# Attention in half-steps, and another order for the last expert group and the final norm

## The chip, the cores and the metric

The kernel runs on one core of a Trainium2 chip. The metric is the device time of one execution in microseconds. TensorE does the matrix products (PE in the rows, PEld for its weight loads), VectorE is DVE, ScalarE is ACT, GpSimd is POOL, and SyncE (SP) issues nearly all transfers. Each engine works through its own instructions in order and waits on semaphores for the others.

## The reference

A trunk of two layers over 256 tokens and 16 meta tokens of width 1024, in float32. Layer 0 mixes with a gated convolution and linear attention, layer 1 with grouped-query attention. Each layer ends with 32 experts, of which each token uses two, and after the last layer comes an RMS norm:

```python
def attend_block(q_blk, k, v):
    s = jnp.einsum('bqhgd,bkhd->bhgqk', q_blk, k) * (ATT_HEAD_DIM ** -0.5)
    p = jax.nn.softmax(s, axis=-1)
    return jnp.einsum('bhgqk,bkhd->bqhgd', p, v)
...
    for e in range(N_EXPERTS):
        he = jax.nn.silu(xt @ w_gate[e]) * (xt @ w_up[e])
        out = out + gates[:, e:e + 1] * (he @ w_down[e]).astype(jnp.float32)
...
    return rms_norm(h, norm_final)
```

Layer 1 has 16 query heads and 4 key heads of 64; its queries are the 256 real tokens, its keys all 272. Each expert has three matrices of 1 MB.

## The kernel before

Tokens lie in three tiles: tile 0 has the 16 meta tokens, tiles 1 and 2 have 128 tokens each. `h` (the residual) and `hn` are [128, 3, 1024] in SBUF. There are eight PSUM banks, `B[0]` to `B[7]`.

**Attention of layer 1** goes over eight pairs of heads `p`. For each pair there are two query tiles `i` and two heads `o`, so four score tiles [128, 272], one in each of `B[0]` to `B[3]`. The four engines' programs are written apart and meet in semaphores:

- TensorE: `att_scores(p)` (L1913) makes the four score tiles, each when `p_exp` says that the exponentials of the pair before have left its bank. `turn_probs(p)` (L1926, L1933) transposes the divided probabilities into `B[4]`, `B[5]` and, for the meta keys, `B[6]`. `att_values(p)` (L1947, L1951) multiplies them with the values into `B[7]`. The loop's order is scores of p+1, turns of p, values of p-1.
- VectorE: `maxima(p)` takes four row maxima (L1324) and, for each tile of queries, scales them (L1328, `s_max`). `invert(p)` inverts the four sums of exponentials (L1334) and multiplies the four tiles of probabilities (L1338, `p_ready`). `meta_out(p)` copies the turned meta part (L1344), `oT_low(p)` makes the low part of the output (L1348). The order is maxima of p+1, low part of p-2, division of p+1, meta part of p. `qT_out(1)`, the copy of the second half of the turned queries (L1315), stands after the first division.
- ScalarE: `exps(p)` makes the four exponentials with their sums (L832), `pT_out(p)` evacuates the turned probabilities (L841), `oT_out(p)` the output (L845). The order is exponentials of p+1, turned probabilities of p, output of p-1.

The output projection follows when the last `oT_low` is done.

**Experts.** `moe(l)` serves both layers. It works on eight groups `q` of four experts, 32 token slots to an expert. For a group TensorE makes the gate and the up product (`gate_up`, L1711), ScalarE takes silu (L733), VectorE multiplies (L1192), TensorE transposes (L1737), ScalarE evacuates (L735), TensorE makes the down product (`down`, L1748), and both halves of its columns are evacuated as `y` (L739 and L1205). `scatter` (L1800) brings a group's result back to the tokens by a product for each half of columns and each tile, and VectorE's `add_tokens` adds it to `h` (L1172, semaphore `h_added`). The products of the scatter use two banks in turn, so each waits for the add two before it. The scatter of a group comes inside the next group; in the last group (`last_quad`) it stands behind the transposes of the last group's product. Scatters go over half 0 of all tiles, then half 1. In layer 0 there are three tiles, so six products and adds, in layer 1 two tiles and four. Each product is two matmuls in the trace.

**Weights.** SyncE issues one transfer for each matrix, through 18 slots of 1 MB, in the fixed order gate, up, down of each group. The four gate matrices of a group are one stage, the four up matrices another, the four down matrices a third. A slot is filled again when `stage_done` says that its last reader is done. For layer 1 the first three transfers are issued when the query projection is done; the next eight wait for

```python
                sp.wait_ge(sem("oT_ps"), 8)
                for i in range(3, 11):
                    unit(1, i)
```

that is, for the last product with the values. After each layer's first round of experts every engine reads how many more rounds there are (`more_rounds`, none here) and branches past their code; on TensorE that branch stands ahead of `last_quad`.

**Final norm** (`norm(4)`). ScalarE squares each tile of `h` over all 1024 columns with a sum (L543) when the tile's last add is done (`wait_h`), VectorE takes the mean and adds epsilon (L869), ScalarE takes the root (L532), VectorE inverts it (L877) and scales the tile by it and by the gain (L887); SyncE stores each tile (L451).

Of the kernel before, what the change touches and what calls it, by code (L numbers as in the profile page):

```python
# [5 lines left out]
def build_program(nc: bass.Bass, A: dict, out: bass.AP):  # L6
# [9 lines left out]
    P = 128  # L16
# [76 lines left out]
    with ctx:  # L93
# [38 lines left out]
        eps_var = sb("eps_var", [P, 3])  # L132
        idx_g = sb("idx_g", [P, 3, 8], u32)
# [205 lines left out]
        def _(sp):  # L339
# [162 lines left out]
        def wait_h(eng, n, i, steps):  # L502

            tiles = len(NORM_TILES[n - 1]) if n else 3
            if n == 0:
                eng.wait_ge(sem("h_in"), 48)
            elif n in (1, 3):
                eng.wait_ge(sem(f"h_mixed{n // 2}"), [3, 2][n // 2] + i + 1)
            else:
                eng.wait_ge(sem(f"h_added{n // 2 - 1}"), steps * NQ * 2 * tiles + (NQ - 1) * 2 * tiles + tiles + i + 1)  # L510
# [8 lines left out]
        def _(act):  # L519
            link = chain(act, "act_chain")  # L520

            def norm(n, steps=None):
# [23 lines left out]
                if n % 2:  # L546
# [276 lines left out]
            def exps(p):  # L823
                for i in range(2):
                    for o in range(2):
                        at = 16 + 16 * (p // 4) + 8 * i + 2 * (p % 4) + o
                        k = 4 * p + 2 * i + o
                        if o == 0:
                            act.wait_ge(sem("s_max"), 2 * p + i + 1)
                        if p >= 2 and i == 0 and o == 0:  # L830
                            act.wait_ge(sem("pT_ps"), 3 * (p - 1))
                        nc.scalar.activation(probs[:, 4 * (p % 2) + 2 * i + o, :], B[2 * i + o][:, 0:T], ACT.Exp,  # L832
                                             bias=att_max[:, k:k + 1], scale=hstat[:, 3, at:at + 1],
                                             accum_out=att_sum[:, k:k + 1]).then_inc(sem("p_exp"), 1)
# [27 lines left out]
        def _(dve):  # L862
# [16 lines left out]
            def scale_tile(n, i):  # L879
# [4 lines left out]
                if i == 0:  # L884
                    dve.wait_ge(sem("gain_in"), {0: 16, 4: 32}[n])
                gain = gain_last if n else gain_first
                nc.vector.scalar_tensor_tensor(hn[0:m, t, :], h[0:m, t, :], stats[0:m, n, 3, t:t + 1], gain[0:m, :],  # L887
                                               ALU.mult, ALU.mult).then_inc(sem("hn_ready"), 1)

            def norm(n):  # L890
                tiles = len(NORM_TILES[n])
                mean_square(n, 0)
                for i in range(tiles):
                    if i + 1 < tiles:
                        mean_square(n, i + 1)
                    scale_tile(n, i)
# [19 lines left out]
            link(nc.vector.memset(hn[:, 0, :], 0.0))  # L916
            nc.vector.memset(stats[:, :, :, :].rearrange("p a b c -> p (a b c)"), 1.0).then_inc(sem("clear"), 1)

            nc.vector.memset(z[:, :, :].rearrange("p a b -> p (a b)"), 0.0).then_inc(sem("clear"), 1)
            norm(0)  # L920
# [144 lines left out]
            def moe(l):  # L1065
# [99 lines left out]
                def add_tokens(base, q):  # L1165

                    for k in range(nadd):
                        half, t = k // NT, tiles[k % NT]
# [13 lines left out]
                def one_round(r, first):  # L1182
# [136 lines left out]
            def maxima(p):  # L1319
                for i in range(2):  # L1320
                    for o in range(2):
                        k = 4 * p + 2 * i + o
                        dve.wait_ge(sem("s_ps"), k + 1)
                        last = nc.vector.tensor_reduce(att_rcp[:, k:k + 1], B[2 * i + o][:, 0:T], X, ALU.max, negate=True)  # L1324
                    link(last)
                    at = 16 + 16 * (p // 4) + 8 * i + 2 * (p % 4)
                    k = 4 * p + 2 * i
                    nc.vector.tensor_tensor(att_max[:, k:k + 2], att_rcp[:, k:k + 2], hstat[:, 3, at:at + 2], ALU.mult).then_inc(sem("s_max"), 1)  # L1328

            def invert(p):  # L1330
                k = 4 * p
                dve.wait_ge(sem("p_exp"), 4 * p + 4)
                dve.wait_ge(sem("s_max"), 2 * p + 2)
                nc.vector.reciprocal(att_rcp[:, k:k + 4], att_sum[:, k:k + 4]).then_inc(sem("p_rcp"), 1)  # L1334
                dve.wait_ge(sem("p_rcp"), p + 1)
                for x in range(4):
                    pr = probs[:, 4 * (p % 2) + x, :]
                    nc.vector.tensor_scalar(pr, pr, att_rcp[:, 4 * p + x:4 * p + x + 1], None, ALU.mult).then_inc(sem("p_ready"), 1)  # L1338
# [677 lines left out]
```

## Time and profile before

| | us |
|---|---|
| median of 3 runs | 763.95 |
| lowest and highest | 762.96, 767.34 |
| the profiled execution, its own time | 761.59 |
| its span, first to last instruction | 759.7 |

In the profiled execution TensorE was busy for 646.2 us (85% of the span), VectorE for 250.0, ScalarE for 172.8, GpSimd for 61.4. The transfers moved 233.91 MB, 308 GB/s on average. The mean granted TensorE clock was 0.937. Times in the rows are counted from the start of the span. In a timeline row the first number is the start, the second the time to the end of the merged instructions, and a square bracket at the end says how long the engine had been idle and what released it. Busy times are of one engine; they overlap those of others, so their sum says nothing.

### The profile page before, as it was taken

To read this page: it belongs to the slowest core of one execution; us is meant where nothing else is said; L and a number is where in the kernel's file an instruction comes from. 1 tells how busy PE (TensorE), PEld (TensorE's weight loads), DVE (VectorE), ACT (ScalarE), POOL (GpSimd) and SP (SyncE) were. 2 spreads that over 40 slices of the span, in tenths; PEclk is the share of its full clock that TensorE was granted. 3 is DMA by queue.
4 is the path that set the end of the run, shared out by engine and by line. 5 is a ranking of instruction groups with operands and counts; after the bars stand their busy time and mean duration, and the time that the engine had idled before them with its cause. 6 is when DMAs were issued, how large, how long until landed. Compare 5 with 4: busy or idle time off the path is not lost.

```text
span 759.7 us, 10990 instructions
## 1 busy us (share of the span) xinstructions
PE 646.2 (85%) x4720; PEld 398.5 (52%) x4720; DVE 250.0 (33%) x575; ACT 172.8 (23%) x354; POOL 61.4 (8%) x43
## 2 busy tenths in 40 slices
PE   3999999988899998699589988787899787686674
PEld 3896987346566373374224345466566353244231
DVE  5255434133122332033043677713213221211204
ACT  5653350031200010010005346713111000000002
POOL 4222260000000000000003420000000000000000
PEclk9999999997999999699799999999899988888888
DMA  9760345991999999999994322069999999999991
GB/s 300 272 219 1 125 125 176 374 421 62 408 422 402 423 420 421 422 420 422 417 395 156 112 75 92 1 198 424 368 424 420 420 421 421 421 420 421 421 392 63
DMA packets 45753, 233.91 MB, mean 308 GB/s; under 512 B 4432, under 2 KB 4688, under 8 KB 23168
## 3 DMA queue, kind: packets, MB, share of 16 engines
q1 hardware_dynamic: 44864, 232.34, 76.5%
q0 software_dynamic: 832, 0.76, 0.7%
q8 instruction: 41, 0.67, 0.4%
q14 instruction: 16, 0.13, 0.0%
HBM read 232.02 MB, written 1.05 MB: 307 GB/s over the span
## 4 chain that ended last, share of the span: by engine, by line
PE 66%; DMA 18%; DVE 6%; SPq 4%; ACT 3%; issue 2%; DVEq 0%; ACTq 0%
PE bank L1711 11%; DMA ring<-in_moe_w_up 10%; PE bank L1775 8%; DMA tail<-in_moe_w_up 7%; PE bank L1800 7%; PE bank L1748 5%; PE bank L1408 5%; PE bank L1409 4%; PE bank L1410 4%; PE bank L1762 4%; SPq L370 4%; PE bank L1617 4%; PE bank L1863 4%; ACT scratch L832 2%; PE bank L1870 1%
## 5 line engine op out<-in xcount | busy, mean ns | idle before, releaser
L1711 PE MATMUL bank<-ring,hnT 128*32 128x256 f32 (+1 forms) x1616 | 141.5, 462 | 56.5 <-DMA ring<-in_moe_w_up 24.8
L1711 PEld LDWEIGHTS bank<-ring,hnT 128*32 128x32 f32 x1616 | 70.7, 128 | 120.8 <-issue 50.9
L1800 PE MATMUL bank<-moe_scratch 128*128 128x512 f32 (+1 forms) x160 | 78.1, 611 | 1.8 <-ACT moe_scratch L739 1.6
L1192 DVE TENSOR_TENSOR moe_scratch<-moe_scratch,bank 128x256 f32<-128x256 f32 x16 | 6.7, 421 | 182.4 <-ACT moe_scratch L733 182.4
L1172 DVE TENSOR_TENSOR h<-bank,h 128x512 f32<-128x512 f32 (+1 forms) x80 | 55.1, 689 | 23.7 <-PE bank L1800 23.7
L1775 PE MATMUL bank<-sel,hn 128*128 128x256 f32 x240 | 59.1, 406 | 0.0
L1748 PE MATMUL bank<-ring,moe_scratch 128*32 128x512 f32 x496 | 58.2, 595 | 0.3 <-ACT moe_scratch L735 0.3
L1775 PEld LDWEIGHTS bank<-sel,hn 128*128 128x128 f32 x240 | 58.0, 337 | 0.0
L1800 PEld LDWEIGHTS bank<-moe_scratch 128*128 128x128 f32 (+1 forms) x160 | 22.7, 169 | 50.3 <-issue 26.3
L1408 PE MATMUL bank<-hnT_hi,mix_hi 128*128 128x272 f32 x160 | 47.1, 294 | 1.7 <-DVE scratch L1016 1.7
L733 ACT ACTIVATE moe_scratch<-bank 128x256 f32<-128x256 f32 x16 | 6.1, 384 | 186.0 <-PE bank L1711 186.0
L1409 PE MATMUL bank<-hnT_hi,mix_lo 128*128 128x272 f32 x160 | 46.3, 289 | 0.0
L1711 PE MATMUL bank<-tail,hnT 128*32 128x256 f32 (+1 forms) x304 | 46.1, 433 | 0.0
L1410 PE MATMUL bank<-hnT_lo,mix_hi 128*128 128x272 f32 x160 | 46.0, 288 | 0.0
L1762 PE MATMUL bank<-sel,hn 128*128 128x128 f32 (+1 forms) x120 | 30.5, 421 | 2.1 <-DVE sel L1122 2.1
L1408 PEld LDWEIGHTS bank<-hnT_hi,mix_hi 128*128 128x128 f32 x160 | 30.3, 189 | 3.6 <-DVE scratch L1016 2.0
L1762 PEld LDWEIGHTS bank<-sel,hn 128*128 128x128 f32 x120 | 29.2, 335 | 5.6 <-issue 5.6
L1410 PEld LDWEIGHTS bank<-hnT_lo,mix_hi 128*128 128x128 f32 x160 | 30.2, 189 | 0.0
L1409 PEld LDWEIGHTS bank<-hnT_hi,mix_lo 128*128 128x128 f32 x160 | 30.2, 189 | 0.0
L307 POOL TENSOR_TENSOR mix_lo<-ring,mix_hi 128x2048 fp32r<-128x2048 f32 x5 | 24.0, 4800 | 69.8 <-ACT mix_hi L586 69.8
L1748 PEld LDWEIGHTS bank<-ring,moe_scratch 128*32 128x32 f32 x496 | 14.9, 109 | 26.8 <-issue 26.0
L739 ACT ACTIVATE moe_scratch<-bank 128x512 f32<-128x512 f32 x16 | 9.6, 597 | 84.8 <-PE bank L1748 84.8
(291 smaller groups left out, 852.0 us busy)
## 6 DMA issues: line engine op xcount, KB each, us to landing
ring<-in_moe_w_down SPq DMA_DIRECT2D x62, 1024.0 KB, 25.9
ring<-in_moe_w_up SPq DMA_DIRECT2D x48, 1024.0 KB, 24.2
ring<-in_moe_w_gate SPq DMA_DIRECT2D x46, 1024.0 KB, 22.1
ring<-in_sc_w_in SPq DMA_DIRECT2D x12, 1024.0 KB, 12.5
tail<-in_moe_w_gate SPq DMA_DIRECT2D x10, 1024.0 KB, 26.2
tail<-in_moe_w_up SPq DMA_DIRECT2D x8, 1024.0 KB, 25.4
ring<-in_moe_w_gate SPq DMA_DIRECT2D x14, 512.0 KB, 9.3
ring<-in_moe_w_up SPq DMA_DIRECT2D x14, 512.0 KB, 10.1
```

The source lines that it names most:

```text
L370: sp.dma_start(dst.rearrange("p (c n) -> p c n", c=KC), src).then_inc(sem(f"weights{l}_{stage_of(i) % NSEM}"), 16)
L1172: nc.vector.tensor_tensor(hh, B[[7, 4][k % 2]][0:n, :], hh, ALU.add).then_inc(sem(f"h_added{l}"), 1)
L1408: mm(dst, left[0], right[0], start=start, stop=False)
L1409: mm(dst, left[1], right[0], start=False, stop=False)
L1410: return mm(dst, left[0], right[1], start=False, stop=stop)
L1617: last = mm(bank[:, :], hnT[:, c, TILE_AT[t]:TILE_AT[t] + P], out_weights(half, c), start=(c == 4), stop=(c == 3))
L1711: return mm(bank[at, :], xT[:, c, mine], right, start=(c == 0), stop=(c == KC - 1))
L1748: last = mm(B[5 + half][at, :], heT[:, c, at], w[j][:, c * D + half * W:c * D + half * W + W], start=(c == 0), stop=(c == 1))
L1762: last = mm(B[k][:, width * cc:width * cc + width], hn[:, t, c:D:KC], picks, start=(t == a), stop=(t == b - 1))
L1775: last = mm(B[k % 2][:, 2 * P * cc:2 * P * cc + 2 * P], hn[:, t, c:D:KC], picks, start=(t == a), stop=(t == b - 1))
L1800: mm(B[[7, 4][k % 2]][0:m, :], selgT[:, TILE_AT[t]:TILE_AT[t] + m], y[:, half, :], start=True, stop=True).then_inc(sem(f"sc_ps{l}"), 1)
L1863: last = mm(bank[:, :], hnT[:, c, TILE_AT[t]:TILE_AT[t] + P], att_weights(2 * b + c // 4)[:, c % 4 * W:c % 4 * W + W], start=(c == 0), sto ...
```

## The change

Attention's steps are cut in two, one half for each tile of queries: `exps(p, i)`, `maxima(p, i)`, `normalize(p, i)` (the former `invert`, now with a reciprocal for each half) and `att_scores(p, i)`. Each engine's loop is written in another order around them. In the last expert group of both layers the scatter of the group before stands between the gate and the up product, its adds stand ahead of the product of silu and up, and the last group's scatter goes tile by tile. The final norm works in halves of 512 columns: squares, scaling and stores; epsilon and the division by 1024 move into the root.

```diff
@@ SyncE, output
             for i in range(2):
-                sp.wait_ge(sem("hn_ready"), HN_BEFORE[4] + i + 1)
-                sp.dma_start(out[0, i * P:(i + 1) * P, :], hn[:, 1 + i, :]).then_inc(sem("out_done"), 16)
-            sp.wait_ge(sem("out_done"), 32)
+                for half in range(2):
+                    cols = slice(half * W, half * W + W)
+                    sp.wait_ge(sem("hn_ready"), HN_BEFORE[4] + 2 * i + half + 1)
+                    sp.dma_start(out[0, i * P:(i + 1) * P, cols], hn[:, 1 + i, cols]).then_inc(sem("out_done"), 16)
+            sp.wait_ge(sem("out_done"), 64)
@@ all engines
+        def scattered(q, tiles):
+            if q < NQ - 1:
+                return [(half, t) for half in range(2) for t in tiles]
+            return [(half, t) for t in tiles for half in range(2)]
@@ ScalarE, final norm
+                if n == 4:
+                    done = steps * NQ * 4 + (NQ - 1) * 4
+                    for i, t in enumerate(tiles):
+                        for half in range(2):
+                            act.wait_ge(sem("h_added1"), done + 2 * i + half + 1)
+                            cols = slice(half * W, half * W + W)
+                            nc.scalar.activation(hn[:, t, cols], h[:, t, cols], ACT.Square,
+                                                 accum_out=(stats[:, 4, 0, t:t + 1], half_ss[:, t:t + 1])[half]).then_inc(sem("norm_ss"), 1)
+                            if i == 1:
+                                act.wait_ge(sem("norm_var"), upto(4) + half + 1)
+                                of = slice(tiles[half], tiles[half] + 1)
+                                nc.scalar.activation(stats[:, 4, 2, of], stats[:, 4, 1, of], ACT.Sqrt,
+                                                     bias=eps_bias[:, 0:1], scale=1.0 / D).then_inc(sem("norm_std"), 1)
+                    return
@@ ScalarE, attention
-            exps(0)
+            exps(0, 0)
+            exps(0, 1)
             qT_out(1)
             for p in range(8):
-                if p < 7:
-                    exps(p + 1)
-                pT_out(p)
                 if p:
                     oT_out(p - 1)
+                if p < 7:
+                    exps(p + 1, 0)
+                pT_out(p)
+                if p < 7:
+                    exps(p + 1, 1)
@@ VectorE, final norm
+                total(0)
+                invert_root(4, 0)
+                dve.wait_ge(sem("gain_in"), 32)
+                scaled(0, 0)
+                total(1)
+                scaled(0, 1)
+                invert_root(4, 1)
+                scaled(1, 0)
+                scaled(1, 1)
@@ VectorE, experts
                     for q in range(NQ):
+                        if q == NQ - 1:
+                            add_tokens(base, q - 1)
                         dve.wait_ge(sem(f"silu{l}"), base + q + 1)
                         nc.vector.tensor_tensor(he, act_g, B[2][:, F:2 * F], ALU.mult).then_inc(sem(f"he{l}"), 1)
-                        if q:
+                        if 0 < q < NQ - 1:
                             add_tokens(base, q - 1)
@@ VectorE, attention
-            maxima(0)
+            maxima(0, 0)
+            maxima(0, 1)
             query_rotate(1, 1)
             query_scale(1)
-            invert(0)
-            qT_out(1)
             for p in range(8):
+                normalize(p, 0)
+                if p:
+                    meta_out(p - 1)
                 if p < 7:
-                    maxima(p + 1)
-                if p >= 2:
-                    oT_low(p - 2)
+                    maxima(p + 1, 0)
+                normalize(p, 1)
+                if p == 0:
+                    qT_out(1)
+                if p:
+                    oT_low(p - 1)
                 if p < 7:
-                    invert(p + 1)
-                meta_out(p)
-            oT_low(6)
+                    maxima(p + 1, 1)
+            meta_out(7)
             oT_low(7)
@@ TensorE, last expert group
-                    gate_up(r, q)
+                    gate_up(r, q, (0,))
+                    scatter(r, q - 1)
+                    gate_up(r, q, (1,))
                     he_transposes(r, q)
-                    scatter(r, q - 1)
                     transpose_weights(r, q)
@@ TensorE, attention
             for p in range(8):
                 if p < 7:
-                    att_scores(p + 1)
-                turn_probs(p)
+                    att_scores(p + 1, 0)
                 if p:
                     att_values(p - 1)
+                if p < 7:
+                    att_scores(p + 1, 1)
+                turn_probs(p)
             att_values(7)
```

In the final norm `total` adds the two halves' sums of squares and `scaled` scales one half of a tile's columns. `wait_h` for the transposes after layer 0 asks for the adds of whole tiles in the new order.

## Rows read from the trace of the kernel before

**Rows 1.** The page, part 2: DMA busy in tenths of 40 slices.
```profile
DMA  9760345991999999999994322069999999999991
```

**Rows 2.** Timeline: first division, seventh product and evacuation, queue's restart.
```profile
457.56 1.18 DVE L1338 TENSOR_SCALAR scratch<-scratch,att_rcp 128x272 f32<-128x272 f32 x4
...
495.79 1.08 PE L1947 MATMUL bank<-scratch 128*64 128x256 f32 x8
...
497.36 0.38 ACT L845 ACTIVATE hnT_hi<-bank 128x256 fp32r<-128x256 f32 x1 [1.31 <-PE bank L1951]
...
499.81 0.33 SPq L367 DMA_DIRECT2D ring<-in_moe_w_gate  x1
```

**Rows 3.** Timeline of one attention step, by engine.
```profile
475.32 0.58 ACT L832 ACTIVATE scratch<-bank,att_max,scratch 128x272 f32<-128x272 f32 x1 [1.42 <-DVE att_max L1328]
...
477.56 1.09 ACT L841 ACTIVATE scratch<-bank 128x512 f32<-128x512 f32 x2
...
477.70 0.18 DVE L1334 RECIPROCAL att_rcp<-att_sum 128x4 f32<-128x4 f32 x1 [1.19 <-ACT scratch L832]
477.92 1.18 DVE L1338 TENSOR_SCALAR scratch<-scratch,att_rcp 128x272 f32<-128x272 f32 x4
479.01 0.41 DVE L1344 COPY scratch<-bank 64x256 f32<-64x256 f32 x1
479.34 0.77 DVE L1324 TENSOR_REDUCE att_rcp<-bank 128x1 f32<-128x272 f32 x2
...
480.23 0.78 DVE L1324 TENSOR_REDUCE att_rcp<-bank 128x1 f32<-128x272 f32 x2
...
479.15 1.09 PE L1926 MATMUL bank<-consts,scratch 128*128 128x128 f32 x8
...
481.59 1.08 PE L1947 MATMUL bank<-scratch 128*64 128x256 f32 x8 [0.78 <-DVE hnT_lo L1348]
```

**Rows 4.** Busy us in attention: PE, PEld, DVE, ACT, POOL, then clock, DMA.
```profile
470.00:480.00 10.00, 8.43 (x74) 5.36 (x72) 7.41 (x27) 7.20 (x22) 0.00 (x0) 1.00 0.00 0
```

**Rows 5.** Timeline, layer 0's last expert group and the work after it.
```profile
377.20 0.64 PE L1711 MATMUL bank<-ring,hnT 128*32 128x256 f32 x2 [3.45 <-DMA tail<-in_moe_w_up]
...
383.58 5.82 PE L1800 MATMUL bank<-moe_scratch 128*16 128x512 f32 x12
...
390.72 0.64 PE L1748 MATMUL bank<-ring,moe_scratch 128*32 128x512 f32 x4
...
407.16 0.29 DVE L1229 TENSOR_TENSOR hnT<-bank,gain_att 128x128 f32<-128x128 f32 x1 [5.46 <-issue]
```

**Rows 6.** Layer 0's last down issue: start, and time to landing.
```profile
L373 SPq DMA_DIRECT2D ring<-in_moe_w_down x1: 2143/2143/2143, 359.7 to 359.7; - x1
...
DMA to landing us min/median/max: 27.4/27.4/27.4
```

**Rows 7.** Timeline of TensorE, layer 1's last up and down products.
```profile
731.34 5.35 PE L1711 MATMUL bank<-ring,hnT 128*32 128x256 f32 x64 [3.96 <-DMA ring<-in_moe_w_up]
...
742.93 3.64 PE L1748 MATMUL bank<-ring,moe_scratch 128*32 128x512 f32 x32
```

**Rows 8.** Chain of waits: an up product warm (start us, us, what).
```profile
585.17 3.50 PE bank L1711 x64
```

**Rows 9.** Stretch in layer 1's last up product, same columns.
```profile
731.50:732.00 0.50, 0.50 (x8) 0.22 (x4) 0.00 (x0) 0.00 (x0) 0.00 (x0) 0.50 1.06 442
```

**Rows 10.** Layer 1's last two down issues: starts, and time to landing.
```profile
L373 SPq DMA_DIRECT2D ring<-in_moe_w_down x2: 436/1283/2130, 710.9 to 713.1; - x2
...
DMA to landing us min/median/max: 27.0/27.5/28.0
```

**Rows 11.** Timeline of VectorE in the final norm.
```profile
752.49 0.15 DVE L869 TENSOR_SCALAR stats<-stats 128x1 f32<-128x1 f32 x1 [0.52 <-ACT hn L543]
...
755.05 1.28 DVE L887 SCALAR_TENSOR_TENSOR hn<-h,stats,ring 128x1024 f32<-128x1024 f32 x1
```

**Rows 12.** The two output stores: time to landing.
```profile
DMA to landing us min/median/max: 2.9/3.0/3.1
```

More of the change, by code:

```diff
@@ L821, in _, with exps @@
             qT_out(0)
[L823 to L834, printed above, removed]
+            def exps(p, i):
+                act.wait_ge(sem("s_max"), 2 * p + i + 1)
+                if p >= 2 and i == 0:
+                    act.wait_ge(sem("pT_ps"), 3 * (p - 1))
+                for o in range(2):
+                    at = 16 + 16 * (p // 4) + 8 * i + 2 * (p % 4) + o
+                    k = 4 * p + 2 * i + o
+                    nc.scalar.activation(probs[:, 4 * (p % 2) + 2 * i + o, :], B[2 * i + o][:, 0:T], ACT.Exp,
+                                         bias=att_max[:, k:k + 1], scale=hstat[:, 3, at:at + 1],
+                                         accum_out=att_sum[:, k:k + 1]).then_inc(sem("p_exp"), 1)
             def pT_out(p):
@@ L884, in scale_tile, with first_norm, last_norm, total @@
                 if i == 0:
-                    dve.wait_ge(sem("gain_in"), {0: 16, 4: 32}[n])
-                gain = gain_last if n else gain_first
-                nc.vector.scalar_tensor_tensor(hn[0:m, t, :], h[0:m, t, :], stats[0:m, n, 3, t:t + 1], gain[0:m, :],
+                    dve.wait_ge(sem("gain_in"), 16)
+                nc.vector.scalar_tensor_tensor(hn[0:m, t, :], h[0:m, t, :], stats[0:m, n, 3, t:t + 1], gain_first[0:m, :],
                                                ALU.mult, ALU.mult).then_inc(sem("hn_ready"), 1)
[L890 to L896, printed above, removed]
+            def first_norm():
+                mean_square(0, 0)
+                for i in range(3):
+                    if i < 2:
+                        mean_square(0, i + 1)
+                    scale_tile(0, i)
+            def last_norm():
+                def total(i):
+                    t = NORM_TILES[4][i]
+                    dve.wait_ge(sem("norm_ss"), upto(4) + 2 * i + 2)
+                    nc.vector.tensor_tensor(stats[:, 4, 1, t:t + 1], stats[:, 4, 0, t:t + 1], half_ss[:, t:t + 1], ALU.add).then_inc(sem("norm_var"), 1)
+                def scaled(i, half):
+                    t = NORM_TILES[4][i]
+                    cols = slice(half * W, half * W + W)
+                    nc.vector.scalar_tensor_tensor(hn[:, t, cols], h[:, t, cols], stats[:, 4, 3, t:t + 1], gain_last[:, cols],
+                                                   ALU.mult, ALU.mult).then_inc(sem("hn_ready"), 1)
+                total(0)
[7 more added lines that the diff above has]
+                scaled(1, 1)
             def transposes_out(n):
@@ L1165, in add_tokens @@
                 def add_tokens(base, q):
-                    for k in range(nadd):
-                        half, t = k // NT, tiles[k % NT]
+                    for k, (half, t) in enumerate(scattered(q, tiles)):
                         n = TILE_N[t]
@@ L1371, in _ @@
             moe(1)
-            norm(4)
+            last_norm()
         @block.tensor
@@ L1790, in scatter @@
                     pe.wait_ge(sem(f"selgT{l}"), r * NQ + q + 1)
-                    for k in range(nadd):
-                        half, t = k // NT, tiles[k % NT]
+                    for k, (half, t) in enumerate(scattered(q, tiles)):
                         m = TILE_N[t]
-                        if k == 0:
+                        if half == 0:
                             pe.wait_ge(sem(f"y_act{l}"), r * NQ + q + 1)
-                        if k == NT:
+                        else:
                             pe.wait_ge(sem(f"y_dve{l}"), r * NQ + q + 1)
```

67 lines of the change are left out of this document (34 added, 33 removed).

## The prediction

> **What bounds the kernel now.** I read the page first, then the queue of the weight loads, then the chain that ended last, then the timeline of three stretches. The page's DMA line [rows 1] shows two long stretches at 9, one for each layer's experts, with an almost idle stretch between: most of the 759.7 us are weights coming in, and no order of instructions shortens them. What can shorten the kernel is what lies between and after: the end of layer 0's experts, the attention of layer 1, and what follows the last weight. The queue that loads layer 1's experts stands still through attention and issues again at 499.81, when the eighth product with the values is done [rows 2]. So a microsecond taken out of attention moves both TensorE and the weight stream of layer 1, and a microsecond taken out of layer 0's end moves them too, since all of attention hangs on it.
>
> **Attention.** In one step (a pair of heads, two query tiles) nothing overlaps well: the four exponentials run from 475.32 to 477.56, then VectorE inverts and multiplies (477.70 to 479.01), copies the meta part (to 479.34), takes the first two maxima, and only then can the next exponentials start; ScalarE sat idle 1.42 us for them [rows 3]. The chain is 2.38 for exponentials to reciprocal, 1.31 for the division, 0.33 for the copy, about 1.0 for two maxima and their scaling: 5.02 us a step.
> After the change a half of VectorE's work can run while ScalarE does the other half. What then bounds a step:
> VectorE's own work: two halves of division, each 0.22 + 2 x 0.273 = 0.765; the copy 0.33; two halves of maxima, each 0.89 (479.34 to 480.23); the low part of the output, about 0.4 [rows 3]. That is 1.53 + 0.33 + 1.78 + 0.36 = 4.0 us. The added reciprocal is in it.
> ScalarE's order makes a ring: product with the values, 1.57 to its evacuation (495.79 to 497.36) [rows 2], 0.3 to issue past it, two exponentials 1.12, the two evacuations of the turned probabilities about 1.0 to 1.1 [rows 3], and the next product may start: 4.1 us.
> TensorE: 8.43 us busy in ten, two steps, so at most 4.2 a step with its modelled ends [rows 4].
> I walked one period through all three queues: the second half's division is done when TensorE is through the values and the second half of scores, so the turns are ready for ScalarE; VectorE has 0.1 us left over. I take 4.15 us a step, between 4.0 (VectorE never waits) and 4.6 (half of the old idle stays).
> The start gets worse, because the copy of the second half of the queries now stands behind half a maximum and a whole second division, and the first turns wait for it: from the division at 457.56 less its reciprocal [rows 2]: 0.77, about 0.4 until scores, 0.89, 0.77, the 0.7 copy, then turns and evacuation and one half of scores, about 2.2: first product with the values at 463.0 (an estimate). Six steps of 4.15 give 487.9, the last step, without scores and maxima in it, about 3.5 (an estimate), and 1.57: the weights' queue would go at 493.0 instead of 499.81, 6.8 us earlier. TensorE is less busy at the start and may be at its lower clock there; I leave 0.4 for it. Attention term: **6.4 us**, from 3.7 (steps of 4.6) to 7.5 (steps of 4.0).
>
> **Layer 0's last expert group.** TensorE was through the gate product 3.45 us before the up weights let it go on at 377.20, and did the scatter of the group before (12 matmuls, 5.82 us) at 383.58, when it stood ahead of the down product at 390.72 [rows 5]. The change puts that scatter into the wait: 373.75 + 5.82 = 379.6, so up starts 2.4 us late. Before, the scatter began 6.38 us after up's start, behind silu, product and transposes; 379.6 + 6.4 + 0.4 for the last evacuation is 386.4 at most. Down's weights, whose last issue is at 359.7 and lands 27.4 later [rows 6], are there at 387.1. So down starts at 387.15 and not 390.72: **3.6 us**, and the weights are the new bound. VectorE's adds move along with the scatter; they stood idle there anyway. The projection's weights follow down's in the same queue, whose order stays; that they keep ahead of it is an estimate. The scatter of the last group in tile order has the same 12 matmuls and 6 adds; the next transposes ask for the fourth add instead of the fifth but stand behind the scatter itself in TensorE's queue, so nothing to 0.3: I take nothing.
> At 731.34, after 3.96 us idle, 64 matmuls took 5.35 us [rows 7]; 64 such matmuls took 3.50 warm [rows 8]; the granted clock there was 0.50, which is 1.2 of 2.4 GHz [rows 9]. A cold start costs 1.85 us. Layer 0's down would follow an idle of about 2 us; bounds 1.75 to 3.6, and I stay at 3.6, as its gap is shorter than the 3.96.
>
> **Layer 1's last expert group.** The same edit. TensorE is free at 731.34 - 3.96 = 727.38, the scatter of 8 matmuls takes two thirds of 5.82, 3.9, and ends at 731.3, just as up lands: it costs nothing. Up stays warm and ends 1.85 earlier. But the last down issue is at 713.1 and lands 28.0 later [rows 10], at 741.1, and before down began at 742.93 [rows 7]. So only 1.8 us can be had of the 4 that the scatter took; and TensorE now idles from about 736.5 to 741.1, longer than the 3.96 that went before the cold block. A cold down costs 1.85 and eats the 1.8: I take **0.0**, from -1.9 to +1.8. The Trainium skill (TensorE: Matmul & The Clock Gate, The HAM clock gate) says that the half rate is the default and that idling brings it back, and warns of gaps spent waiting on DMA; the trace agrees with 0.50. By that rule alone this term is about 0 as well; without it it would be 1.8.
>
> **Final norm and output.** Before, after the last add VectorE idled 0.52 and began at 752.49, and its second whole-tile scaling began at 755.05 and took 1.28, to 756.33; the output landed 3.0 later [rows 11, 12]. In tile order the first tile's adds are both done two adds sooner, so its squares no longer wait. Walk: sum of halves at 752.5, root and reciprocal to 753.1, then half scalings of about 0.6 with the second total between: starts at 753.1, 753.8, 754.6, 755.2, end near 755.9: 0.45 less. The last store carries half a tile; of 3.0 us I give 0.4 back. **0.9 us**, from 0.2 to 1.4. The memset of the bias at the start lies under the input loads.
>
> **Sum.** 3.6 + 6.4 + 0.0 + 0.9 = 10.9 us. The profiled execution took 761.59 (span 759.7), so its like would take 750.7. The median of the runs is 2.36 above the profiled one; from the median 763.95 - 10.9 = **753.0 us**.
>
> **Rivals.**
> Steps that overlap less (15%): every wait across engines in the new order adds up, steps of 4.6: 2.7 less, 755.8. For it: three bounds within 0.2 of each other leave no slack. Against it: the walk closes.
> Layer 0's gain is lost (10%): after layer 0 VectorE stood 5.46 us with no releaser shown before it worked at 407.16 [rows 5], while the weights were still streaming. If that stall ends with the stream and not 5.46 after the last add, TensorE's projection waits for VectorE: 3.3 lost, 756.3.
> A stall of that kind at layer 1's end (8%): both layers end in the same branch, and VectorE stood 0.52 there against 5.46 in layer 0. The changed amount of VectorE code may put the place after the branch where it isn't loaded: up to 5.46 - 0.52 = 4.9 more right ahead of the norm, 757.9. Beside it the Trainium skill (Runtime: NRT & Kernel Launch, Instruction fetch mechanics) says that a taken branch whose target is outside the loaded pages stalls the engine; layer 0's 5.46 fits, 0.52 would be a target at hand.
> More than forecast (10%): down isn't cold and the steps reach 4.0: 10.9 + 1.8 + 1.1 = 13.7, 750.2.
> Nothing gained (4%): attention keeps its 5.02 and VectorE's stall takes layer 0's part: 762 or so.
> Slower (3%): the halves line up into one chain, because ScalarE's output copy now stands ahead of the exponentials and the turns wait for both halves. A step is then two halves of about 3 (scores, maxima, exponentials, division) and the turn, evacuation and product, about 3.5 more: 9.5 us, seven steps of 4.5 more, less 4.5 gained elsewhere: 791. It decides from steps of 5.7 us on (0.64 x 7 = 4.5); above 6.2 it would be measured as slower.
> The forecast itself: 50%.
>
> **Numbers.** 0.5%, 3.8 us, is about what a measurement of this kernel tells from none. All cases but the last two (and little of the others) gain more: faster 0.93, same 0.04, slower 0.03. Range: the steps' and the clock's bounds and the two stalls reach from 750 to 758; the median's own distance to a profiled run adds at the low end: 748.5 to 758.
>
> **What would show it.** Exponentials following each other at 4.0 to 4.3 us, the weights' queue going again some 10 us earlier than 499.81, layer 0's down 3.6 us sooner and right at its weights' landing; layer 1's down about 9.8 us behind up's landing, at clock 0.5; two stores a tile. I am wrong if the steps stay above 4.6, if VectorE's stall at a layer's end grows, or if down doesn't wait for its weights.

## The result and the profile after

The median of the changed kernel is 759.99 us (756.4 to 762.5, 18 runs), that of the kernel before 763.79 us (759.52 to 767.34, 18 runs): a ratio of 0.9949, 95% interval 0.9932 to 0.9965. That is 3.9 us faster, against a forecast of 10.9, and outside the range of 748.5 to 758.0. The profiled execution took 757.3 (span 755.5, mean clock 0.94), 4.2 of span less than before; the accounts below are between the two profiled executions. Where they are held against medians, I say so. Cold and warm stand for a product that ran, wholly or in part, at granted clock 0.50, and for one at 1.00.

The page after, part 2, DMA busy by slice, for [rows 1]:

```profile
DMA  9760345991999999999995313079899999999991
```

The idle stretch between the layers is there as before. **Layer 0's last group**, timeline of the kernel after, for [rows 5]:

```profile
367.04 5.78 PE L1761 MATMUL bank<-ring,hnT 128*32 128x256 f32 x64 [5.47 <-DMA ring<-in_moe_w_gate]
372.64 5.81 PE L1849 MATMUL bank<-moe_scratch 128*16 128x512 f32 x12
378.39 0.41 PE L1761 MATMUL bank<-ring,hnT 128*32 128x256 f32 x2
...
387.68 5.69 PE L1798 MATMUL bank<-ring,moe_scratch 128*32 128x512 f32 x32 [3.79 <-DMA ring<-in_moe_w_down]
...
402.71 3.70 PE L1920 MATMUL bank<-ring,hnT 128*128 128x512 f32 x8
406.51 0.29 DVE L1277 TENSOR_TENSOR hnT<-bank,gain_att 128x128 f32<-128x128 f32 x1 [5.90 <-issue]
...
407.25 3.70 PE L1920 MATMUL bank<-ring,hnT 128*128 128x512 f32 x8 [0.83 <-DVE hnT L1282]
```

The same stretch by windows (length in us, then busy us of PE, PEld, DVE, ACT, POOL, then clock, DMA share, GB/s), and the last down issues of layer 0, for [rows 6]:

```profile
386.00:387.50 1.50, 0.00 (x0) 0.00 (x0) 0.00 (x0) 0.00 (x0) 0.00 (x0) 0.50 1.03 385
387.50:390.00 2.50, 2.32 (x12) 0.68 (x16) 0.00 (x0) 0.00 (x0) 0.00 (x0) 0.50 1.06 388
390.00:392.00 2.00, 2.00 (x16) 0.55 (x12) 0.00 (x0) 0.00 (x0) 0.00 (x0) 0.53 1.05 387
392.00:393.40 1.40, 1.37 (x16) 0.17 (x8) 0.00 (x0) 0.00 (x0) 0.00 (x0) 1.00 1.05 386
```

```profile
L375 SPq DMA_DIRECT2D ring<-in_moe_w_down x2: 2133/2135/2137, 357.3 to 359.5; - x2
...
DMA to landing us min/median/max: 26.9/27.5/28.1
```

The scatter fills the wait for up, and down starts when its weights land (359.5 + 28.1 = 387.6), 3.04 us sooner than before. But TensorE had idled 3.79 us, its clock was at 0.50 (1.2 of 2.4 GHz), and the product took 5.69 instead of 3.64. VectorE's stall behind the layer is 5.90 instead of 5.46, and TensorE waits 0.83 for it in the projection instead of 0.18. The first score comes at 451.90 instead of 452.56: of the forecast's 3.6 us, 0.66 is left. From down's end to the first score it is 58.5 us (58.2 before).

**Attention**, timeline of the kernel after: TensorE through one step, then ScalarE's last output and the queue's restart, for [rows 2, 3]:

```profile
467.19 0.73 PE L1962 MATMUL bank<-scratch 64*128 64x272 f32 x4
...
467.85 1.08 PE L1996 MATMUL bank<-scratch 128*64 128x256 f32 x8
...
468.76 0.60 PE L2000 MATMUL bank<-scratch 128*64 128x256 f32 x4
...
469.30 0.73 PE L1962 MATMUL bank<-scratch 64*128 64x272 f32 x4
...
469.96 1.09 PE L1975 MATMUL bank<-consts,scratch 128*128 128x128 f32 x8
...
470.98 0.63 PE L1982 MATMUL bank<-consts,scratch 128*32 128x128 f32 x8
...
471.54 0.73 PE L1962 MATMUL bank<-scratch 64*128 64x272 f32 x4
...
494.75 0.33 SPq L369 DMA_DIRECT2D ring<-in_moe_w_gate  x1
...
494.76 0.38 ACT L867 ACTIVATE hnT_hi<-bank 128x256 fp32r<-128x256 f32 x1 [1.60 <-PE bank L2000]
```

A stretch of it by windows, for [rows 4]:

```profile
480.00:490.00 10.00, 10.00 (x86) 5.99 (x84) 8.88 (x31) 8.49 (x27) 0.00 (x0) 1.00 0.01 2
```

A step takes 471.54 - 467.19 = 4.35 us (before 5.02), and TensorE has no gap in it: 10.00 of 10 us busy, against 8.43 before. From the first score to the restart it is 42.85 us instead of 47.25: 4.4 gained, 6.4 forecast.

**Layer 1's end**, timeline of the kernel after, for [rows 7, 11]:

```profile
726.90 3.89 PE L1849 MATMUL bank<-moe_scratch 128*128 128x512 f32 x8
730.72 3.66 PE L1761 MATMUL bank<-ring,hnT 128*32 128x256 f32 x64
...
737.48 3.64 PE L1798 MATMUL bank<-ring,moe_scratch 128*32 128x512 f32 x32 [1.41 <-DMA ring<-in_moe_w_down]
...
745.82 0.69 DVE L1218 TENSOR_TENSOR h<-bank,h 128x512 f32<-128x512 f32 x1 [0.17 <-PE bank L1849]
...
749.30 0.16 DVE L926 TENSOR_TENSOR stats<-stats,half_ss 128x1 f32<-128x1 f32 x1 [2.79 <-issue]
749.49 0.29 ACT L579 ACTIVATE stats<-stats,eps_bias 128x1 f32<-128x1 f32 x1 [3.08 <-DVE stats L926]
```

Up is warm, down follows an idle of only 1.41 us and is warm as well. Then, after its last add, VectorE stands for 2.79 us with no releaser (before it was 0.52, put down to ScalarE's squares), and the norm waits for it. From down's end to the end of the span it is 14.4 us instead of 13.1.

The account, in spans: layer 0's end 0.66 + attention 4.4. The queue restarts 5.06 us sooner, but its last down issue comes 3.98 us sooner (709.09 against 713.07), so 1.1 is lost while the weights stream. Last down issue to down's end is 32.03 instead of 33.51: 1.5 gained. Less 1.3 behind it: 4.2.

### The profile page after: what moved, and what is told of

The parts are those of the page before. It is cut to its first block, busy times and chain, and to the rows that moved or that the text cites. A ratio compares the mean times of both kernels' runs of the same rounds, so it can differ in the third digit from the quotient of the medians.

```text
span 755.5 us, 11041 instructions
## 1 busy us (share of the span) xinstructions
PE 645.6 (85%) x4720; PEld 397.1 (53%) x4720; DVE 252.4 (33%) x586; ACT 173.6 (23%) x358; POOL 61.4 (8%) x43
## 4 chain that ended last, share of the span: by engine, by line
PE 68%; DMA 18%; SPq 6%; DVE 3%; issue 2%; ACT 1%; DVEq 0%; ACTq 0%
PE bank L1761 9%; PE bank L1825 8%; DMA ring<-in_moe_w_down 7%; DMA ring<-in_moe_w_up 7%; PE bank L1849 6%; PE bank L1798 6%; PE bank L1458 5%; SPq L372 5%; PE bank L1459 4%; PE bank L1460 4%; PE bank L1812 4%; PE bank L1667 4%; PE bank L1913 4%; DMA tail<-in_moe_w_up 4%; SPq L375 2%
## 5 line engine op out<-in xcount | busy, mean ns | idle before, releaser
L1761 PE MATMUL bank<-ring,hnT 128*32 128x256 f32 (+1 forms) x1616 | 137.4, 450 | 51.0 <-DMA ring<-in_moe_w_up 22.2
L1761 PEld LDWEIGHTS bank<-ring,hnT 128*32 128x32 f32 x1616 | 68.9, 125 | 110.4 <-issue 45.2
L1798 PE MATMUL bank<-ring,moe_scratch 128*32 128x512 f32 x496 | 60.3, 613 | 5.6 <-DMA ring<-in_moe_w_down 5.2
L1667 PE MATMUL bank<-ring,hnT 128*128 128x512 f32 x64 | 28.3, 597 | 0.3 <-ACT hnT L706 0.3
```

Of the source, the lines that this page charges most:

```text
L1667: last = mm(bank[:, :], hnT[:, c, TILE_AT[t]:TILE_AT[t] + P], out_weights(half, c), start=(c == 4), stop=(c == 3))
L1761: return mm(bank[at, :], xT[:, c, mine], right, start=(c == 0), stop=(c == KC - 1))
L1798: last = mm(B[5 + half][at, :], heT[:, c, at], w[j][:, c * D + half * W:c * D + half * W + W], start=(c == 0), stop=(c == 1))
```

## The experiments

"First score" is the first score matmul of attention, which carries all of layer 0's end; "stall" is VectorE's idle time with no releaser behind a layer's last add.

**1. VectorE's branch moved.** The changed kernel, but VectorE branches before its last group's adds, where it waits anyway:

```diff
-                one_round(0, True)
+                one_round(0, True, range(NQ - 1))
@@ in the loop of further rounds
+                        one_round(r, False, range(NQ - 1, NQ))
...
+                one_round(more, False, range(NQ - 1, NQ))
```

> The changed kernel, with VectorE's branch past the code of further rounds moved ahead of the last expert group, in both layers, so that it falls into a wait for weights. Theory (the idle times of 5.9 us in layer 0 and 2.8 us in layer 1 with no releaser are code loading after the branch): both are gone from the place behind the last add, the final norm's first total starts within 0.6 us of the last add, layer 0's projection no longer waits 0.83 for VectorE; the end comes some 3 us sooner than in the changed kernel, near 752.5 us of span. Rival (VectorE has work of its own there, or the semaphore of the squares is late): both stay, and the time is that of the changed kernel.

Median 754.29 (753.01 to 757.5), ratio 0.9893 [0.9863, 0.9923]; span 751.2. VectorE in the timeline of this kernel, behind layer 0 and then behind layer 1:

```profile
401.37 0.29 DVE L1281 TENSOR_TENSOR hnT<-bank,gain_att 128x128 f32<-128x128 f32 x1 [1.58 <-PE bank L1907]
...
745.01 0.15 DVE L926 TENSOR_TENSOR stats<-stats,half_ss 128x1 f32<-128x1 f32 x1
```

Both stalls are gone: in layer 0 VectorE now waits 1.58 us for TensorE's product, in layer 1 not at all. By the ratios 4.3 us (0.0056 of 764), and 4.3 of span too, hung on the place of one branch; the intervals do not overlap. Of the span, 2.9 lie behind layer 1's down (11.5 us to the end, not 14.4) and 1.1 between layer 0's down and the first score (57.4, not 58.5).

What the stall holds is seen in the transfers of the changed kernel. From 746.0 to 749.4, the end of the last add and the stall behind it, the DMA queues move nothing but one packet, of a queue that the profile calls "instruction":

```profile
DMA  0000000000000000020000000000000000000000
...
q14 instruction: 1, 0.01, 0.6%
```

It moves at 747.5, 1.0 us after the last add, and VectorE works again 1.5 us after its end. In layer 0's stall such a packet moves only at 404.5, 3.9 us after the last add, between 356 GB/s of weights (400.5 to 406.6), and VectorE works again 1.7 us after its end: the longer stall there is mostly a longer wait for this packet. In the kernel before one moves at 753.1, 1.1 us behind layer 1's last add, when VectorE had been at work since 752.49. So the branch is followed by a load of instructions in both, and only in the changed kernel VectorE has to wait for it.

**2 and 3. Attention alone, and everything but attention.** Experiment 2 is the kernel before with the attention hunks of the diff; experiment 3 is the changed kernel without them.

> The kernel before with the half-steps of attention alone. If attention's gain is its own: first prefetch to the restart of the weights' queue takes 45.9 us as in the changed kernel, not 50.3, steps are 4.35 us, and the time is 4 to 4.5 us below before. Rival (the steps profit from the other parts): less than 3.

> The changed kernel with attention as before: last expert group, last scatter, final norm and output. If the parts add up: about the time of before, within 1 us: layer 0 gives 0.65, layer 1's last group 1.4, the stall ahead of the final norm takes 2.3 and the halves give 1. Rival (the stall hangs on how much code VectorE has, and attention's half-steps bring most of the added instructions): no stall at the final norm here, 3 us below before.

Attention alone: median 761.59 (757.7 to 766.45), 0.9982 [0.9957, 1.0008], span 760.2. The rest alone: 761.01 (759.13 to 764.57), 0.9974 [0.9951, 0.9998], span 757.7. Steps are 4.35 us in the one and 5.02 in the other. The stall at layer 1's end, in the timelines of experiment 2 and then 3:

```profile
753.81 0.22 DVE L872 TENSOR_SCALAR stats<-stats 128x1 f32<-128x1 f32 x2 [2.77 <-issue]
```

```profile
750.50 0.16 DVE L925 TENSOR_TENSOR stats<-stats,half_ss 128x1 f32<-128x1 f32 x1 [0.51 <-issue]
...
752.87 0.16 DVE L925 TENSOR_TENSOR stats<-stats,half_ss 128x1 f32<-128x1 f32 x1 [0.90 <-issue]
```

It comes with attention's half-steps, though they lie 250 us earlier: of VectorE's code only a part far in front of the branch has changed. Experiment 2 misses the 4 to 4.5 us that were expected of it, and its interval holds 1: the steps and the restart are as expected, the stall takes its part back. Experiment 3 has no stall, as its rival said, but gains 2.0 us by its ratio and not 3. In experiment 3 the norm in halves gains nothing by itself: last add to the end is 7.7 us, as before, and in its middle a second idle of 0.90 without a releaser appears. The execution from which the account starts was an early one in layer 0: up could go on at 377.20, but only at 379.38, 380.74 and 379.27 in experiments 2, 8 and 10, which have the same order. So 0.66 needs a fairer measure. The gate product of the last group, ahead of everything that the new order moves, began at 367.21 before and at 367.04 in the changed kernel, and at 368.94, 370.93 and 368.76 in those three. From there to the first score it is 84.9 us in the changed kernel, 85.4 before, and 85.7, 86.0 and 85.5 in the three: the new order has 0.5 to 1.1.

**4. Layer 0's gap filled.** The changed kernel with three products ahead of the last down of layer 0, whose result nobody reads:

```diff
                     transpose_weights(r, q)
+                    if l == 0:
+                        for _ in range(3):
+                            mm(B[0][:, :], ident, consts[:, 128:640], start=True, stop=True)
                     down(r, q)
```

> The changed kernel, with three products of 512 columns that nobody reads in TensorE's queue ahead of layer 0's last down product (about 2.6 us of the 3.8 that it idles there). Theory (down ran at 1.2 GHz because of that idle): down takes 3.65 and not 5.7 us, and everything up to the transposes after layer 0 comes 2 us sooner; but VectorE's 5.9 us without a releaser start 2 us sooner too, so if those are a fixed time the gain carries over into the projection, and if they end with the weight stream the gain is lost there. Rival (down is slow because weights are still landing): down stays at 5.7 us.

Median 758.47 (754.17 to 762.28), 0.9945 [0.9917, 0.9972]; span 752.3. Timeline of this kernel:

```profile
384.15 2.84 PE L1881 MATMUL bank<-consts 128*128 128x512 f32 x6
387.79 3.64 PE L1798 MATMUL bank<-ring,moe_scratch 128*32 128x512 f32 x32 [0.81 <-DMA ring<-in_moe_w_down]
...
404.61 0.29 DVE L1277 TENSOR_TENSOR hnT<-bank,gain_att 128x128 f32<-128x128 f32 x1 [5.95 <-issue]
```

With the gap filled, down takes 3.64 us instead of 5.69, and the first score comes at 450.00, 1.9 sooner. VectorE's stall keeps its length (5.95) and moves along, so it does not eat the gain as my rival had it. But the median is that of the changed kernel (0.9945 against 0.9949). So the cost is shown in this pair of executions, not in the medians; the profiled one of experiment 4 (754.17) was the fastest of its ten.

**5. Both.** Experiments 1 and 4 together.

> The changed kernel with both: VectorE's branch ahead of the last expert group, and the three unread products ahead of layer 0's down. Theory: the two gains add, since one is time of TensorE ahead of the transposes after layer 0 and the other the wait behind them; a span of about 749, some 6 us under the changed kernel, and a ratio to before near 0.984. Rival (one limit stands behind both, the weights of the projection): no better than the better of the two alone, 751.

Median 754.15 (752.11 to 755.44), 0.9868 [0.9841, 0.9895]; span 752.3, where 749 was expected. Layer 0's down took 3.64 us, but the first score, 449.76, is only 0.2 sooner than in experiment 1, since its weights landed 1.4 later; and layer 1's down took 5.34 after an idle of 2.15. Against experiment 1 the intervals overlap: a gain of the fill is not shown here either.

**6 and 7. What bounds a step.** The changed kernel; experiment 6 makes the last score tile of a step twice, experiment 7 lets VectorE copy a spare 128x128 tile in six of the eight steps. Neither result is read.

```diff
@@ 6, att_scores
+                    if i and o:
+                        mm(B[2 * i + o][:, 0:T], qT1[rows, p, i * P:(i + 1) * P], kT1[rows, p // 2, :], start=True, stop=True)
@@ 7, oT_low
+                if p < 6:
+                    nc.vector.tensor_copy(spare, consts[:, 128:256])
```

> The changed kernel in which TensorE makes the last of the four score tiles of each pair twice, once unread: two more matmuls of 272 columns, about 0.23 us a step. If TensorE bounds the step of 4.35 us, the steps grow by that, to 4.58. Rival (the ring through ScalarE bounds it, or VectorE): they stay at 4.35 or grow by less than 0.1.

> The changed kernel with one more VectorE copy of 128 columns in each of the first six attention steps, ahead of its wait for ScalarE's evacuation of the output. If TensorE bounds the step, the copy falls into VectorE's idle 0.36 us and the steps stay at 4.35. Rival (VectorE bounds it, as its 4.0 us of work forecast): they grow by the copy's 0.1 to 0.2.

One execution each, 759.07 and 760.71 us. TensorE in the timeline of experiment 6 (L1963 is the repeated product), and a stretch of experiment 7 by windows:

```profile
473.92 0.49 PE L1964 MATMUL bank<-scratch 64*128 64x272 f32 x1
473.93 0.49 PE L1963 MATMUL bank<-scratch 64*128 64x272 f32 x1
474.26 0.39 PE L1964 MATMUL bank<-scratch 64*128 64x272 f32 x1
474.26 0.39 PE L1963 MATMUL bank<-scratch 64*128 64x272 f32 x1
474.49 0.62 PE L1964 MATMUL bank<-scratch 64*128 64x272 f32 x2
475.04 1.09 PE L1977 MATMUL bank<-consts,scratch 128*128 128x128 f32 x8
```

```profile
474.00:483.00 9.00, 9.00 (x78) 5.36 (x78) 8.51 (x33) 7.51 (x24) 0.00 (x0) 1.00 0.00 0
```

More work for TensorE lengthens every step, from 4.35 to 4.81; more for VectorE lengthens none (4.35), though it is busy 95% of the time. TensorE bounds the step. Twice the 0.23 that I had expected was added: the two heads' score products run side by side in the rows, and a third tile has no partner; its two matmuls stand alone for 0.55 us. The times themselves compare badly: experiment 7's start of attention ran at clock 0.66 and its layer 1 down took 5.34, neither of which the copy can be blamed for.

**8. The moved branch in the kernel before.**

> The kernel before with VectorE's branch ahead of the last expert group. Theory: the stall after layer 0 is gone (5.46 us idle before) but TensorE waited only 0.18 for VectorE there, and layer 1 had none to lose, so the time is that of before within 1 us; ScalarE and VectorE only start earlier. Rival (the stall also held something else): 2 us or more faster.

Median 765.87 (761.92 to 767.57), 1.0017 [0.9995, 1.0039]; span 764.4. VectorE's wait in layer 0 falls from 5.46 to 1.79, and nothing is gained. The move is no gain of its own: it takes out a stall, and before, the one at layer 1's end was 0.52. Layer 0's stall alone brings next to nothing when it goes, because little of it was exposed: TensorE had waited only 0.18 for it. From down's end to the first score it is 58.2 us before and 57.75 here; in the changed kernel and experiment 1, 58.5 and 57.4. So the stall cost 0.45 in the one and 1.1 in the other.

**9 and 10. The other parts taken out.** Experiment 9 is experiment 1 with the final norm, its stores and the last scatter's order as before; experiment 10 is the changed kernel with the last group's order (scatter behind the transposes) as before.

> As e1_branch, but the last scatter, the final norm and the output as before the change. With no code loading in the way, the last down product's end to the end of the span is then 13.1 us as before, less the 0.2 to 0.5 of VectorE's idle time; in e1_branch it was 11.5. So the halves give about 1.3 us. Rival (the halves' gain comes from the stores): the time from the last add to the first store differs by less than 0.3.

> The changed kernel without the new order of the last expert group (gate, up, transposes, scatter, as before); attention, last scatter and final norm stay changed. Theory (in layer 0 the new order brings 3 us down's start sooner and loses 2 of them to a cold down, in layer 1 it brings 1.4): this one is 2 us slower than the changed kernel, down takes 3.64 us in both layers and starts without idle time before it. Rival (what the order gains is all lost): same time.

Experiment 9: median 758.3 (757.4 to 760.29), 0.9925 [0.9894, 0.9955], span 757.8. Last add to the end is 7.45 us, against 6.12 in experiment 1: once nothing stalls, the halves are worth 1.3, near the 0.9 of the forecast. By the ratios the kernel is 2.4 us slower than experiment 1, though the intervals overlap. Part of that is no work of the norm's: its two last downs were cold, 5.84 and 5.96 after idles of 3.63 and 3.83; experiment 1's were 5.28 and 3.64. Layer 1's:

```profile
739.03 5.96 PE L1759 MATMUL bank<-ring,moe_scratch 128*32 128x512 f32 x32 [3.83 <-DMA ring<-in_moe_w_down]
```

Experiment 10: median 760.67 (758.52 to 761.71), 0.9949 [0.9931, 0.9967], span 756.6. The ratio is the changed kernel's own, where 2 us slower were expected. So the new order of the last group is worth 1.1 us of span in one pair and, in medians, nothing to within some 2 us.

**11 and 12. Towards a better kernel.** Experiment 11 is experiment 1 with fills before down in both layers (three and one) and three before the wait for the second tile of turned queries. Experiment 12 also copies the second half of the queries right after the first half of the first division:

```diff
                 normalize(p, 0)
                 if p:
                     meta_out(p - 1)
+                else:
+                    qT_out(1)
                 if p < 7:
                     maxima(p + 1, 0)
                 normalize(p, 1)
-                if p == 0:
-                    qT_out(1)
```

> As e5_branch_fill, with one unread product ahead of layer 1's last down too and three between the two tiles of the second transposition of queries at the start of attention, where TensorE idles 2.9 us. Theory (what attention's start and layer 1's down lose in some executions is the half clock after an idle stretch): first score to first evacuation of an output takes 12.3 us and not 14.3, layer 1's down 3.64 and not 5.34; some 2 us under e5_branch_fill on average, ratio to before near 0.984. Rival (the unread products only take time): no change or slower.

> As e11_fills, with VectorE's copy of the second half of the queries in the idle time ahead of the first half maximum instead of behind the second division. Theory (the first turns waited for that copy): first score to first evacuation of an output 0.6 us shorter than in e11_fills. Rival (the scores it now delays are as late): unchanged.

Medians 753.78 (751.06 to 755.55), 0.9852 [0.9822, 0.9881], and 752.03 (750.15 to 755.54), 0.9843 [0.9814, 0.9871]; spans 752.9 and 750.0. Experiment 12 has the best median: by the ratios 12.0 us under the kernel before and 8 under the changed one. Against experiments 1, 5 and 11 the intervals overlap, so the moved branch is what is shown of it; the 2 us expected of experiment 11 against experiment 5 are not. The clock through attention's start, from 15 us of each, kernels after, 1 and 12:

```profile
451.90:466.90 15.00, 10.51 (x74) 6.68 (x76) 12.02 (x39) 9.27 (x26) 0.00 (x0) 0.89 0.53 170
```

```profile
450.00:465.00 15.00, 10.52 (x62) 6.54 (x63) 11.05 (x36) 8.35 (x23) 0.00 (x0) 0.77 0.53 168
```

```profile
450.20:465.20 15.00, 13.18 (x90) 7.79 (x92) 13.23 (x44) 10.72 (x30) 0.00 (x0) 1.00 0.53 173
```

First score to first output evacuation was 13.17, 14.20 and 11.73 us in these, and 12.26 in experiments 4 and 11 at clock 1.00. The start's length goes with the clock; the earlier copy gives 0.5 more. One fill before layer 1's down was too little: in experiment 12 it was still slow after a further idle of 3.80, and in experiment 11 it took 6.46 after 3.78.

```profile
733.16 5.34 PE L1802 MATMUL bank<-ring,moe_scratch 128*32 128x512 f32 x32 [3.80 <-DMA ring<-in_moe_w_down]
```

## Why the prediction missed

The direction held, both of the whole and of every part but the last, and the sum was 6.7 us too large in span. By its own terms:

**Layer 0's end, 3.6, measured 0.66 (0.5 to 1.1 counted from the group's gate product).** The failed step is "layer 0's down would follow an idle of about 2 us". My own walk gave it away: up's 64 products from 379.6 would end near 383, down could not start before 387.1, and only a few short transposes lie between. The 6.38 us that it used from up's start to the scatter were those of an up that had itself started cold (377.20 to 382.18 [rows 5], 4.98 us); behind the moved scatter up was warm, 378.39 to 382.05. So the new order took the cold start from up, where it was not counted as a gain, and gave it to down, which waits for its weights either way. The idle was 3.79, nearly as long as the 3.96 that I had used as the mark of a cold start, and 2.05 us were lost to clock 0.50. The landing came within 0.5 of 387.15. The Trainium skill (TensorE: Matmul & The Clock Gate, The HAM clock gate), which I had weighed in layer 1 only, warns of just such gaps spent on DMA; this trace agrees, 5.69 against 3.64. The rest is VectorE's stall, which costs 1.1 here and cost 0.45 before (0.65 more), and the scatter in tile order, which gives 0.3: 3.04 - 2.05 - 0.65 + 0.3 = 0.6. The rival that the stall would end with the stream fell, since in experiment 4 it moved along and kept its length; but a part of it became exposed.

**Attention, 6.4, measured 4.4.** The step that failed is TensorE's bound, "8.43 us busy in ten, at most 4.2 a step". Busy time was that of the old order, with four score tiles together. Those take 1.14 us there, from the start of this row of the timeline of before to that of the turns at 479.15 [rows 3]:

```profile
478.01 1.19 PE L1913 MATMUL bank<-scratch 64*128 64x272 f32 x8
```

Cut in two they take 0.66 each, 0.18 more in all, so a step is 4.35: the sum of TensorE's own work, as experiments 6 and 7 show. Five steps at 0.2 are 1.0 us; the last two took 4.08 and 3.88 for my 4.15 and 3.5, 0.3 more; the start took 13.17, where my walk to 463.0 and 1.57 more had 12.0 and I added 0.4 for the clock: 0.8 more. VectorE's and ScalarE's bounds held, both have slack.

**The stream between, not in the sum.** I let the 6.8 us at the restart reach the end undiminished. From restart to last down issue it took 214.34 us against 213.26, and in the other ten timed kernels 213.3 to 214.3. The changed kernel's first product of layer 1's experts took 4.40 us against 3.64 before. Over all profiled executions the two go together: where that product took 3.64 (before, experiments 5, 6, 7, 8 and 12) the way was 213.3 to 213.7, where it took 4.14 to 4.45 (the changed kernel, 1 to 4, 9 to 11) 213.6 to 214.3. That fits a loss of up to 1 us to a cold first product, but no run changed it by itself, and I leave the cause open.

**Layer 1's last group, 0.0, measured +1.5.** The two opposed parts were right, but the cold down did not come here: the weights were only 1.41 us behind TensorE. In four others of the new order (experiments 1, 3, 4 and 6) the idle was 0.25 to 1.39 and down took 3.64, in five (5, 7, 9, 11 and 12) 2.15 to 3.83 and down took 5.3 to 6.5. The term swings between my ends with where the stream stands, and in the changed kernel's profile it fell well: that is luck, not the forecast.

**Final norm, 0.9, measured -1.3.** The halves are worth 1.3 (experiments 9 and 1), the stall took 2.3 more than before. I had this rival at 8% and 4.9 us; it came with 2.3, less than layer 0's stall, and experiment 2 ties it to attention's code, experiment 1 to the branch. The Trainium skill (Runtime: NRT & Kernel Launch, Instruction fetch mechanics) says that a taken branch to a place outside the loaded pages stalls the engine; the runs agree, with the stall gone in experiment 1 and one instruction packet moving inside it in the changed kernel. I should have given it more than 8%: two visits to the same kind of branch showed 5.46 and 0.52, and the change put new VectorE code in front of them. The 0.52 was also a wait for ScalarE by the row, so it said little about how near a stall was.

**The rivals.** Steps above 4.6 did not come, nor the chain of halves that would have been slower. "Nothing gained" (762) lies nearer to the time than the forecast, but not for its reason, since the steps did get shorter. What came was a mixture of small shortfalls: 2.9 in layer 0, 2.0 in attention, 1.1 in the stream and 2.2 at the end, against 1.5 won in layer 1. The two largest terms, layer 0's and attention's, both stood above the middle of their own bounds (1.75 to 3.6, and 3.7 to 7.5), and the stall behind the last add and the loss in the stream stood in the sum with nothing.

## What to carry to other kernels

Pulling work out of a product's shadow into an earlier wait leaves the gap somewhere else: add up how long TensorE then idles before the next product, and price it cold if an idle of that length was followed by a cold product anywhere in the trace. Take an engine's bound from its instructions in the new grouping, not from busy time in the old one. And look behind every branch that an engine takes after its last work of a stage: put it inside a wait, since any edit to code ahead of it can open a stall there.

## What was not expected of the hardware

- VectorE's stall behind the branch depends on where it stands and on code far away: 0.52 before, 2.79 after (2.62 to 3.00 in experiments 4, 6, 7 and 10), 2.77 with attention's edit alone, 0.51 without it; in layer 0, while weights stream (356 GB/s in the changed kernel), 4.7 to 6.0. With the branch moved into a wait it was gone in both layers.
- The length of the gap alone does not say what the next product will cost. In layer 0, gaps of 3.63, 3.79, 4.21 and 4.31 us were followed by a down of 5.84, 5.69, 5.28 and 5.21 (experiment 9, the changed kernel, experiments 1 and 6), the longer gap by the shorter product. In layer 1, 2.15 and 2.60 us were followed by 5.34, one of 1.41 by 3.64; in experiment 5 the clock was still 1.00 when that down began at 735.45, and 0.51 from 735.8 to 739.2: it fell inside the product.
- Two score products of 64 rows, one for each head, run side by side; a single one more costs 0.46 us a step, four fifths of the 0.57 that a pair takes in the row of eight above (1.14 for two pairs).
